# Issuing each 512-wide split product as two 256-wide matmuls per term

## The chip, the cores and the metric

The kernel runs on one core of a Trainium2 chip. The metric is the device time of one execution in microseconds (us), taken as the median of repeated runs. Of the engines, TensorE carries nearly all of this kernel's work: in the profile its matmuls stand as PE and its loads of the stationary operand as PEld. VectorE is DVE, ScalarE is ACT, GpSimd is POOL and SyncE is SP.

## The reference, cut to what matters

The reference is a two-layer encoder trunk on a sequence of 1024 tokens with 1024 features, all in float32:

```
h = h + mixer_ab(rmsnorm(h, g1), ...)      # layer 0: projections, chunked attention, output projection
h = h + dense_swiglu(rmsnorm(h, g2), ...)  # (silu(h @ w_gate) * (h @ w_up)) @ w_down, 2816 hidden
h = h + mixer_c(rmsnorm(h, g1), ...)       # layer 1: gated MLP with 128x128 position mixing
h = h + moe_swiglu(rmsnorm(h, g2), ...)    # top-2 of 8 experts, 3584 hidden each
return rmsnorm(h, final_norm)
```

Nearly all of the arithmetic is in products of an activation matrix with a weight matrix.

## The kernel before, in words

A float32 matrix product is computed from operands that are split in two. ScalarE copies a tile into a high part of type fp32r (`hi_part`, L271, tile `wh` of the raw weights `wraw`), and VectorE subtracts that from the original to give a low part (`lo_part`, L275, tile `wl`). Activations are split in the same manner, into `xh`/`xl` for the projections, `xdh`/`xdl` and `ah`/`al` for the dense layer, `exh`/`exl` and `mah`/`mal` for the experts. The helper `product` then issues three matmuls into one PSUM bank: high times high (L280), high times the low part of the moving operand (L281), and low stationary times high moving (L282). The first two have the same stationary tile of 128 by 128. The kernel issues no load of the stationary tile by itself; every matmul brings its own, which the profile shows as one PEld row for each PE row.

The stages follow one another on TensorE: value projection (`values_pe`, the moving operand is 512 columns of the weights), key and query projections (`half_pe`, 512 tokens), attention steps with further calls of `half_pe` between them (`attend_pe`), output projection (`out_proj_pe`), the dense layer in two halves of 512 tokens (`gate_up_pe` and `down_pe` with n = 512), the gated MLP (`mix_pe`), routing (`route_pe`), and then the experts one after another (`item_pe`, with the same `gate_up_pe` and `down_pe`). The number of tokens n that an expert's products move is one of `WIDTHS` = 240, 256, 272, 288, 304, 336, 384; `by_width` runs one loop over experts for each width. In this input the widths 240 (three experts), 256 (two), 288 (two) and 304 (one) occur. No expert's product is 512 columns wide, and the position mixing in `mix_pe` moves 128.

`gate_up_pe` is a hardware loop whose body holds four weight units of eight products each; `down_pe` has a loop of four units of eight products, with the first and the last units outside it. In `down_pe` the hidden tile is selected by a register, and the program computes the addresses on TensorE's sequencer. Weights come on SP's queue in units of 128 by 1024 into four slots; a slot is freed by `unit_used`, which the last matmul of a unit increments.

Of the kernel before, what the change touches and what calls it, by code (L numbers as in the profile page):

```python
# [58 lines left out]
def build(nc, io):  # L59
    ctx = ExitStack()  # L60
    with ctx:
# [211 lines left out]
        def lo_part(dve, q, j):  # L273
            dve.wait_ge(hi_done, 4 * q + j + 1)
            dve.tensor_tensor(wl[:, j], wraw[:, j], wh[:, j].bitcast(F32),  # L275
                              ALU.subtract).then_inc(lo_done, 1)

        def product(pe, out, a_hi, a_lo, b_hi, b_lo, first, last):

            pe.matmul(out, a_hi, b_hi, start=first, stop=False)  # L280
            pe.matmul(out, a_hi, b_lo, start=False, stop=False)  # L281
            return pe.matmul(out, a_lo, b_hi, start=False, stop=last)  # L282

        def wtile(w, j, k):
            return w[:, j, k * P:(k + 1) * P]
# [52 lines left out]
        def proj_qk_pe(pe, q, j, b, ready=None, order=tuple(range(KD))):  # L338
            pe.wait_ge(lo_done, 4 * q + j + 1)
            for half in range(2):  # L340
                c = slice(half * HALF, half * HALF + HALF)
                for i, k in enumerate(order):
                    if ready:
                        ready(half, i)
                    mm = product(pe, bank(b + half), wtile(wh, j, k), wtile(wl, j, k), xh[:, k, c], xl[:, k, c],
                                 i == 0, i == KD - 1)
                mm.then_inc((bank_full, unit_used)[half], 1)
# [31 lines left out]
        def values_pe(pe):  # L379
            for g in range(2):  # L380
                for j in range(4):
                    pe.wait_ge(lo_done, j + 1)
                    for kk in range(2):
                        k = 2 * j + kk
                        pe.wait_ge(n_lo, 8 * g + k + 1)
                        for t in range(4 * g, 4 * g + 4):
                            c = slice(t * P, t * P + P)
                            w = slice(512 * kk, 512 * kk + 512)
                            mm = product(pe, bank(t), xh[:, k, c], xl[:, k, c], wh[:, j, w], wl[:, j, w], k == 0, k == KD - 1)
                            if k == KD - 1 and t < 4 * g + 3:  # L390
                                mm.then_inc(v_mm, 1)
                    if g == 1 and j < 3:
                        mm.then_inc(unit_used, 1)
                    elif j == 3:
                        mm.then_inc((v_mm, unit_used)[g], 1)

        def half_pe(pe, u, half, b, ks, used=1):

            c = slice(half * HALF, half * HALF + HALF)
            for k in ks:  # L400
                mm = product(pe, bank(b), wtile(wh, u % 4, k), wtile(wl, u % 4, k), xh[:, k, c], xl[:, k, c], k == 0, k == KD - 1)
            if KD - 1 in ks:
                if half == 0:
                    mm.then_inc(first_half, 1)
                else:
                    mm.then_inc(unit_used, used)
# [1323 lines left out]
```

## Time and profile before

| quantity | before |
|---|---|
| median of 3 runs | 3862.95 us (3862.63 to 3863.59) |
| span of the profiled execution, first to last instruction | 3857.8 us |
| PE busy | 3631.9 us, 94% |
| PEld busy | 3247.7 us, 84% |
| DVE busy, ACT busy | 1724.7 us, 1645.1 us |
| PE matmuls, and weight loads | 24240, 24240 |

No separate time is recorded for the profiled execution: its span is 5.2 us less than the median, and that is what lies around it. Matmuls are pipelined, so the duration of one (its start to its modelled end) is longer than the distance from its start to the start of the next. A duration of 394 ns and a distance of 233 ns stand beside each other in one stage; how fast TensorE works is told by the distance alone. In a view by windows, the figure in brackets counts the instructions that touch the window.

### The profile page before, as it was taken

The numbers are of one execution on the slowest core, as the hardware profiler recorded it, in microseconds if no ns is written. First come the engines' busy times: TensorE is split into PE (matmuls) and PEld (weight loads), VectorE is DVE, ScalarE is ACT, GpSimd is POOL, SyncE is SP. The second block draws the span as 40 slices with busy tenths as digits, with TensorE's granted clock in tenths as the row PEclk, the third lists the DMA queues.
The fourth block names the chain that finished last, engine by engine and source line by source line (L and its number), as shares of the span: only waits on it lengthen the run. The fifth ranks groups of instructions, "written<-read, shape, count | busy, mean of one in ns | idle before, by whom it ended". The sixth has DMA issues, their size and how long they took to land.

```text
span 3857.8 us, 66155 instructions
## 1 busy us (share of the span) xinstructions
PE 3631.9 (94%) x24240; PEld 3247.7 (84%) x24240; DVE 1724.7 (45%) x2452; ACT 1645.1 (43%) x2290; POOL 100.0 (3%) x132
## 2 busy tenths in 40 slices
PE   8999899998999889977999999999999999999993
PEld 5777668886888677747999999999999999999993
DVE  4455433323332433344545555455554544544444
ACT  3455323323332322134546555564654544544542
POOL 1000000000000000010000000000000000000001
PEclk9999999999999999988999999999999999999997
DMA  5111312222222210146666666666565555555446
GB/s 173 34 52 42 115 55 92 92 93 71 93 96 94 104 55 33 55 81 201 193 205 191 206 193 198 201 191 206 191 195 175 164 166 177 164 167 171 158 155 235
DMA packets 150283, 533.85 MB, mean 138 GB/s; under 512 B 17976, under 2 KB 18016, under 8 KB 149936
## 3 DMA queue, kind: packets, MB, share of 16 engines
q1 hardware_dynamic: 126288, 459.86, 36.7%
q0 software_dynamic: 14624, 55.52, 4.0%
q10 hardware_dynamic: 9280, 17.24, 1.5%
q8 instruction: 60, 0.98, 0.1%
q14 instruction: 31, 0.25, 0.0%
HBM read 502.93 MB, written 33.28 MB: 139 GB/s over the span
## 4 chain that ended last, share of the span: by engine, by line
PE 91%; DVE 3%; ACT 2%; DMA 2%; issue 1%; POOL 0%; ACTq 0%; POOLq 0%; DVEq 0%
PE ps L280 29%; PE ps L282 28%; PE ps L281 28%; PE ps L329 1%; PE ps L521 1%; PE ps L506 1%; PE ps L1285 1%; PE ps L460 1%; DMA y<-yrow_d,slot 0%; PE ps L1314 0%; PE ps L541 0%; PE ps L529 0%; PE ps L1079 0%; DVE rstd L311 0%; DMA tok_d<-tokid,slot 0%
## 5 line engine op out<-in xcount | busy, mean ns | idle before, releaser
L275 DVE TENSOR_TENSOR wl<-wraw,wh 128x1024 fp32r<-128x1024 f32 x860 | 1052.1, 1224 | 1558.1 <-ACT wh L271 1558.1
L271 ACT ACTIVATE wh<-wraw 128x1024 fp32r<-128x1024 f32 x860 | 904.4, 1057 | 1197.5 <-PE ps L282 1189.1
L280 PE MATMUL ps<-exh,wh 128*128 128x240 f32 (+3 forms) x3584 | 1021.1, 285 | 11.9 <-issue 9.6
L282 PE MATMUL ps<-exh,wl 128*128 128x240 f32 (+3 forms) x3584 | 1022.2, 285 | 0.0
L281 PE MATMUL ps<-exl,wh 128*128 128x240 f32 (+3 forms) x3584 | 1018.6, 284 | 0.0
L280 PEld LDWEIGHTS ps<-exh,wh 128*128 128x128 f32 x3584 | 679.1, 189 | 12.8 <-issue 12.8
L281 PEld LDWEIGHTS ps<-exl,wh 128*128 128x128 f32 x3584 | 678.4, 189 | 0.0
L282 PEld LDWEIGHTS ps<-exh,wl 128*128 128x128 f32 x3584 | 677.5, 189 | 0.0
L282 PE MATMUL ps<-mah,wl 128*128 (+4 forms) x1792 | 510.5, 285 | 0.0
L280 PE MATMUL ps<-mah,wh 128*128 (+4 forms) x1792 | 509.8, 284 | 0.6
L281 PE MATMUL ps<-mal,wh 128*128 (+4 forms) x1792 | 509.2, 284 | 0.0
L280 PEld LDWEIGHTS ps<-mah,wh 128*128 128x128 f32 x1792 | 338.9, 189 | 2.5 <-issue 2.5
L282 PEld LDWEIGHTS ps<-mah,wl 128*128 128x128 f32 x1792 | 337.9, 189 | 0.0
L281 PEld LDWEIGHTS ps<-mal,wh 128*128 128x128 f32 x1792 | 337.8, 189 | 0.0
L843 ACT ACT_TABLE_LOAD x134 | 171.9, 1283 | 293.9 <-PE ps L282 270.1
L280 PE MATMUL ps<-xdh,wh 128*128 128x512 f32 x704 | 280.9, 399 | 14.9 <-DVE xdl L316 14.9
L281 PE MATMUL ps<-xdl,wh 128*128 128x512 f32 x704 | 279.1, 396 | 0.0
L282 PE MATMUL ps<-xdh,wl 128*128 128x512 f32 x704 | 279.1, 396 | 0.0
L280 PE MATMUL ps<-xh,wh 128*128 128x512 f32 x608 | 249.4, 410 | 19.5 <-DVE xl L773 5.6
L281 PE MATMUL ps<-xl,wh 128*128 128x512 f32 x608 | 243.5, 401 | 0.0
L282 PE MATMUL ps<-xh,wl 128*128 128x512 f32 x608 | 243.2, 400 | 0.0
L280 PEld LDWEIGHTS ps<-xdh,wh 128*128 128x128 f32 x704 | 132.5, 188 | 54.2 <-issue 14.7
(282 smaller groups left out, 3763.3 us busy)
## 6 DMA issues: line engine op xcount, KB each, us to landing
wraw<-in_w_expert SPq DMA_DIRECT2D x676, 512.0 KB, 3.9
wraw<-in_w_main SPq DMA_DIRECT2D x184, 512.0 KB, 3.2
yrow_d<-yst ACTq DMA_DIRECT2D x16, 512.0 KB
yT<-in_xT POOLq DMA_DIRECT2D x4, 1024.0 KB, 11.3
hT<-in_xT POOLq DMA_DIRECT2D x1, 4096.0 KB, 15.3
h_d<-hT POOLq DMA_DIRECT2D x1, 4096.0 KB, 13.2
hT<-h_d POOLq DMA_DIRECT2D x1, 4096.0 KB, 12.4
xrow_d<-rows ACTq DMA_DIRECT2D x16, 256.0 KB, 2.6
```

The source lines that it names most:

```text
L271: act.activation(wh[:, j], wraw[:, j], ACT.Copy).then_inc(hi_done, 1)
L275: dve.tensor_tensor(wl[:, j], wraw[:, j], wh[:, j].bitcast(F32), ALU.subtract).then_inc(lo_done, 1)
L280: pe.matmul(out, a_hi, b_hi, start=first, stop=False)
L281: pe.matmul(out, a_hi, b_lo, start=False, stop=False)
L282: return pe.matmul(out, a_lo, b_hi, start=False, stop=last)
L329: pe.matmul(sums(n), ones[:], sq[:, k % 2], start=k == 0, stop=k == KD - 1).then_inc(n_squ, 1)
L460: mm = pe.matmul(ps[:, starts[h] + a * P:starts[h] + b * P], (qAh, qAh, qAl)[part][hp, tc], key, start=part == 0, stop=part == 2)
L506: mm = pe.transpose(ps[:, o:o + P], eA[:, h, kk * P:kk * P + P], ident[:])
L521: mm = pe.matmul(Y_OUT[h * HD:h * HD + HD], v, ptA[:, kk, h], start=kk == 0, stop=kk == na - 1)
L843: act.activation(buf[:, par, 0:n], bank(par, n), ACT.Silu).then_inc(silu_done, 1)
L1285: mm = pe.transpose(bank(k % 4, P, P * s_), xg[:, s_, k * P:k * P + P], ident[:])
```

## The change

`product` still computes the same three terms in the same order into the same bank. When the moving operand has 512 columns, each term is issued as two matmuls of 256 columns, to the two halves of the bank, with the same stationary tile. Any other width is issued as before. Only the very first matmul of a sum carries `start`, and only the last `stop`.

```
+        COLS = 256
+
         def product(pe, out, a_hi, a_lo, b_hi, b_lo, first, last):
 
-            pe.matmul(out, a_hi, b_hi, start=first, stop=False)
-            pe.matmul(out, a_hi, b_lo, start=False, stop=False)
-            return pe.matmul(out, a_lo, b_hi, start=False, stop=last)
+            n = b_hi.shape[-1]
+            w = COLS if n == 2 * COLS else n
+            for part in range(3):
+                a, b = ((a_hi, b_hi), (a_hi, b_lo), (a_lo, b_hi))[part]
+                for c in range(0, n, w):
+                    s = slice(c, c + w)
+                    mm = pe.matmul(out[:, s], a, b[:, s], start=first and part == 0 and c == 0,
+                                   stop=last and part == 2 and c + w == n)
+            return mm
```

On TensorE, at the head of the dense layer's gate and up loop, two products of the kernel before stand as follows (`xdh` and `xdl` are the split activations, `wh` and `wl` the split weights):

```order
L280 MATMUL ps<-xdh,wh 128x512
L281 MATMUL ps<-xdl,wh 128x512
L282 MATMUL ps<-xdh,wl 128x512
L280 MATMUL ps<-xdh,wh 128x512
L281 MATMUL ps<-xdl,wh 128x512
L282 MATMUL ps<-xdh,wl 128x512
```

With the change the same two products, on the same engine at the same place, are these (x2 is two alike in a row):

```order
L288 MATMUL ps<-xdh,wh 128x256 x2
L288 MATMUL ps<-xdl,wh 128x256 x2
L288 MATMUL ps<-xdh,wl 128x256 x2
L288 MATMUL ps<-xdh,wh 128x256 x2
L288 MATMUL ps<-xdl,wh 128x256 x2
L288 MATMUL ps<-xdh,wl 128x256 x2
```

Six matmuls have become twelve, in the same order of terms, and nothing else was moved. In the dense layer's down loop the tiles `ah` and `al` are picked by a register. Before, the first product of a hidden tile on TensorE reads:

```order
L280 ISA
L280 MATMUL ps<-ah,wh 128x512
L281 REGISTER_ALU
L281 MATMUL ps<-al,wh 128x512
L282 MATMUL ps<-ah,wl 128x512
```

With the change it reads, at the same place of the down loop on TensorE:

```order
L288 ISA
L288 MATMUL ps<-ah,wh 128x256
L288 ISA
L288 MATMUL ps<-ah,wh 128x256
L288 REGISTER_ALU
L288 MATMUL ps<-al,wh 128x256
L288 REGISTER_ALU
L288 MATMUL ps<-al,wh 128x256
L288 MATMUL ps<-ah,wl 128x256 x2
```

The second half of each operand has an address of its own to compute, so the two sequencer instructions of a hidden tile have become four, beside twice as many matmuls.

## Rows read from the trace of the kernel before

**Rows 1.** The page: busy time, and the chain that ended last.

```profile
PE 3631.9 (94%) x24240; PEld 3247.7 (84%) x24240; DVE 1724.7 (45%) x2452; ACT 1645.1 (43%) x2290; POOL 100.0 (3%) x132
...
PE 91%; DVE 3%; ACT 2%; DMA 2%; issue 1%; POOL 0%; ACTq 0%; POOLq 0%; DVEq 0%
```

**Rows 2.** Groups by line and shape, PE: busy, mean ns of one | idle before.

```profile
L280 PE MATMUL ps<-xdh,wh 128*128 128x512 f32 x704 | 280.9, 399 | 14.9 <-DVE xdl L316 14.9
...
L281 PE MATMUL ps<-xl,wh 128*128 128x512 f32 x608 | 243.5, 401 | 0.0
...
L280 PE MATMUL ps<-exh,wh 128*128 128x256 f32 x896 | 247.6, 276 | 1.1 <-DVE wl L275 1.1
...
L281 PE MATMUL ps<-al,wh 128*128 x256 | 100.9, 394 | 0.0
...
L281 PE MATMUL ps<-wl,xh 128*128 128x512 f32 x192 | 77.3, 403 | 0.0
...
L281 PE MATMUL ps<-al,wh 128*128 128x512 f32 x96 | 37.8, 394 | 0.0
```

**Rows 3.** The timeline of PE in the dense layer, 512 columns.

```profile
1000.01 0.39 PE L280 MATMUL ps<-xdh,wh 128*128 128x512 f32 x1
1000.24 0.39 PE L281 MATMUL ps<-xdl,wh 128*128 128x512 f32 x1
1000.48 0.39 PE L282 MATMUL ps<-xdh,wl 128*128 128x512 f32 x1
```

**Rows 4.** The timeline of PE in an expert, 256 columns.

```profile
2600.02 0.28 PE L280 MATMUL ps<-exh,wh 128*128 128x256 f32 x1
2600.13 0.28 PE L281 MATMUL ps<-exl,wh 128*128 128x256 f32 x1
2600.24 0.28 PE L282 MATMUL ps<-exh,wl 128*128 128x256 f32 x1
```

**Rows 5.** Windows in which PE never stops: busy (x count) of each engine.

```profile
core 0: us, PE busy (x) PEld busy (x) DVE busy (x) ACT busy (x) POOL busy (x), PEclk, DMA share, GB/s
446.00:470.00 24.00, 24.00 (x105) 19.34 (x104) 8.01 (x10) 2.13 (x2) 0.00 (x0) 1.00 0.21 66
560.00:780.00 220.00, 220.00 (x944) 176.38 (x943) 73.60 (x79) 73.87 (x88) 0.00 (x0) 1.00 0.29 95
790.00:860.00 70.00, 70.00 (x302) 56.12 (x301) 17.09 (x17) 13.76 (x13) 0.00 (x0) 1.00 0.29 97
45.00:65.00 20.00, 20.00 (x90) 16.39 (x89) 16.26 (x21) 6.88 (x12) 4.31 (x7) 1.00 0.25 58
1346.00:1372.00 26.00, 26.00 (x115) 21.36 (x114) 11.20 (x16) 7.40 (x9) 1.05 (x2) 1.00 0.24 81
1800.00:1900.00 100.00, 100.00 (x885) 100.00 (x884) 56.91 (x74) 61.14 (x83) 0.00 (x0) 1.00 0.62 195
2490.00:2620.00 130.00, 130.00 (x1150) 130.00 (x1149) 74.73 (x96) 80.30 (x109) 0.00 (x0) 1.00 0.61 193
2628.00:2660.00 32.00, 32.00 (x285) 32.00 (x284) 14.59 (x13) 12.59 (x12) 0.00 (x0) 1.00 0.63 196
3240.00:3390.00 150.00, 150.00 (x1128) 150.00 (x1127) 76.13 (x96) 80.86 (x106) 0.00 (x0) 1.00 0.50 163
```

**Rows 6.** Who PE waited for: us in total, times, longest.

```profile
PE ps L280 <- DVE xdl L316: 14.9, 7, 6.5
...
PE ps L280 <- issue: 9.6, 2, 6.2
...
PE ps L521 <- ACT ptA L657: 9.4, 7, 2.8
```

**Rows 7.** Groups by line, PEld: the loads of the dense layer's gate and up.

```profile
L280 PEld LDWEIGHTS ps<-xdh,wh 128*128 128x128 f32 x704 | 132.5, 188 | 54.2 <-issue 14.7 <-DVE xdl L316 7.7
```

**Rows 8.** DMA queues from 1985 to 2470 us, and in the whole span.

```profile
q1 hardware_dynamic: 25029, 91.14, 58.8%
q0 software_dynamic: 928, 3.15, 2.0%
q10 hardware_dynamic: 1088, 2.10, 1.3%
...
q8 instruction: 60, 0.98, 0.1%
```

## The prediction

> **What bounds the kernel now.** I read the page first. PE is busy for 3631.9 of 3857.8 us, DVE and ACT for less than half, and 91% of the chain that ended last is PE [rows 1]. So the time is the time in which TensorE gets through its matmuls, and the change has to be costed in matmuls of two widths.
>
> The groups by shape give the count. Each of the three lines of `product` has 704 matmuls of 512 columns on `xdh` or `xdl`, 608 on `xh` or `xl`, 256 + 96 on `ah` or `al`, and 192 with the weights moving [rows 2]. That is 1856 products, three times 1856 = 5568 matmuls of 512 columns, out of 24240. The rest are the experts' and the small ones, which the change leaves alone.
>
> The same groups tempt to a wrong price. One matmul of 512 columns lasts 394 to 403 ns and one of 256 lasts 276 [rows 2], and by these two for one would cost about 150 ns more, or some 840 us in all. But these are durations from start to modelled end and they overlap. The timeline shows a start every 0.23 us in the dense layer [rows 3] and every 0.11 us in an expert of 256 columns [rows 4]. The distance between starts is what counts.
>
> To get it finer than the timeline I take windows in which PE never stops [rows 5]. An instruction is counted in a window if it touches it, so the distance is (length of the window + duration of one) / count:
>
> - Dense gate and up, 512 columns: 220.394 / 944 = 233.5 ns. Dense down: 70.394 / 302 = 233.1 ns. I take 233.4.
> - Output projection, 512 columns of `xh`: 24.4 / 105 = 232.4 ns.
> - Weights moving, 512 columns: 20.4 / 90 = 226.7 ns in layer 0, 26.4 / 115 = 229.6 in layer 1. I take 228.2.
> - Expert of 256 columns: gate and up 130.276 / 1150 = 113.3 ns, down 32.276 / 285 = 113.2.
> - Expert of 240 columns: 100.277 / 885 = 113.3 ns. Expert of 288: 150.297 / 1128 = 133.2 ns.
>
> Two things are to be seen in them. The 256-wide matmul comes every 113.3 ns, and twice that is 226.6, less than the 233.4 of one 512-wide. And at 240 columns the distance is no smaller than at 256, while PEld is busy for the whole window there, against 176.38 of 220 us at 512. Something that comes once for each matmul, most likely the load of the stationary tile, sets a floor of 113.3 ns.
>
> **The change part by part.** It removes 5568 matmuls of 512 columns and adds 11136 of 256, each with its load. No row shows a 256-wide pair on one stationary tile in a split product, but its parts are shown. L280 and L281 already follow each other on the same stationary tile `wh`, and the 256-wide windows hold these steps with the others: the mean over all three is 113.3 ns, and in the timeline the step from L280 to L281 is the same 0.11 us as the one from L281 to L282 [rows 4]. So I price the pair at 2 x 113.3 = 226.6 ns.
>
> - Dense layer: 3 x (704 + 352) = 3168 matmuls, each 233.4 - 226.6 = 6.8 ns less: 21.5 us.
> - `xh` moving: 3 x 608 = 1824, each 232.4 - 226.6 = 5.8 ns less: 10.6 us. Some 500 of these stand in the attention steps (`half_pe` is called there for 21 half units of 8 products, 504 matmuls), where a gain may turn into waiting for `ptA`; that wait is 9.4 us in total now, in 7 places [rows 6], and 500 x 5.8 ns = 2.9 us is all that could be lost so. I take off 1.
> - Weights moving: 3 x 192 = 576, each 1.6 ns less: 0.9 us.
>
> The sum is 32 us less. Against the profiled execution that gives 3857.8 - 32 = 3826 us of span, and with the 5.2 us around it 3831 for the median.
>
> The bounds of the pair: below, the nearest row is the floor that 240 columns share with 256, and the pair has two loads, so 226 is the least that a row supports; if the gain also reaches the weight-moving products and 233.5 holds for `xh`, it is some 8 ns each, 45 us. Above, the 288-wide row: a line through 288 (133.2 ns) and 512 (233.4) rises by 100.2 / 224 = 0.447 ns for a column and gives 118.9 at 256, so a pair of 237.8. I take the measured 256 since it is the width itself, with the same operand types, helper and loop, in gate and up as well as in down.
>
> The page "TensorE: Matmul & The Clock Gate" of the Trainium skill, section "The mechanism" (of packing small matmuls), says that a load of weights overlaps with running matmuls only when it goes to another group of rows. By that each added load would stand in the open, as in the last rival below. The trace disagrees: in the 256-wide window PE and PEld are both busy for all 130 us [rows 5], and 113.3 ns between starts is less than the 188 ns that one load lasts [rows 7].
>
> Costed at nothing: the sequencer instructions of the down loop double together with its matmuls, and the experts' down loop has the same ratio at 113.2 ns between starts [rows 5]. The waits stay where they are, since every increment sits on the last matmul of the same unit. The end of a sum, which DVE and ACT wait for, comes at 113 + 276 = 389 ns after the start of the last pair, against 394. The clock is granted in full (1.00) at 256 columns as at 512 [rows 5]. Weights are asked for at 95 GB/s in the dense layer and 193 in the experts, so the queue has room for a TensorE that goes 3% faster. The norms that PE waits for (14.9 us, [rows 6]) are DVE's and stay.
>
> **The rivals.**
>
> *The cost goes by columns.* The 512-wide matmul takes 0.456 ns for a column where the experts' 256 takes 0.443. If that 3% belongs to how the tiles lie in memory and not to the width, the 256-wide halves take 116.7 ns each and nothing changes: 3863. For it speaks that at one width the distance differs between stages (226.7, 229.6, 232.4, 233.4), so that placement has a say. Against it, that gate and up and down of the 256-wide expert, on different tiles, agree to 0.1 ns.
>
> *A fixed cost for each matmul.* This is the line above: 118.9 ns at 256 columns. The 3168 then cost 4.4 ns more each, 13.9 us; the 1824 cost 5.4, 9.8 us; the 576 cost 9.6, 5.5 us. Together 29 us slower: 3892. It decides as soon as a half comes at more than 116.7 ns. For it: both 288 and 512 lie on such a line, and so does common sense about issuing twice as often. Against it: the 256-wide row is 5.6 ns under the line. The same page of the Trainium skill, section "Back-to-back issue gap", gives a warm distance of N / 2.4 + 2.5 ns; as an estimate from it a pair of 256 costs 2.5 ns more than one of 512, 14 us over all 5568, which is this rival in a smaller size. Its 215.8 ns for 512 columns is not what the window shows.
>
> *The loop bodies become too long.* The gate and up loop turns 11 times for each half, 20 turns back in all, and its body doubles in matmuls. If each turn back had to fetch code anew, the nearest price is the 6.2 us of the longest "issue" wait [rows 6], which stands where TensorE goes over to the loop of the next width: 20 x 6.2 = 124 us, 3987. Against it: from 1985 to 2470 us TensorE runs two more whole experts of 240 columns, a loop body much longer than that one, and no packet of the instruction queue q8 stands among the queues of that stretch, with 60 in the whole span [rows 8]. The Trainium skill's page "Runtime: NRT & Kernel Launch", section "Instruction fetch mechanics", speaks of a window of two pages and of a stall at a branch out of it; these rows show no such refetch.
>
> *The added load is exposed after all*, because both halves use the tile that is in the array. 5568 x 188 ns [rows 7] = 1047 us, 4910. L280 and L281 share a tile and show nothing of it [rows 4].
>
> **How the numbers follow.** Forecast 0.60, by columns 0.15, fixed cost 0.17, loop bodies 0.06, exposed load 0.02. The likeliest case by itself lies between 3816 (45 us and a little) and 3844 (placement takes away half). The range has to take in no change and, to hold 8 in 10, the nearer half of the fixed cost: 3815 to 3886. A difference of 0.2%, 7.7 us, is about what the measurement can tell from no change. Faster by more: nearly all of the forecast and a little of the column case, 0.61. Same: 0.15. Slower: 0.24.
>
> **What the changed profile would show.** PE x29808 and PEld x29808. In the dense layer's windows one 256-wide matmul every 113.3 ns, PEld busy for the whole window as in the experts, and the two halves of the dense layer about 11 us shorter each. If the distance there is 116 to 117, the column case holds; at 119 the fixed cost. Gaps at the turn of the gate and up loop with q8 packets between them would show the third rival. The experts' stretch should keep its length. Wrong would be the forecast if the 256-wide expert tiles owe their 113.3 ns to their place in memory.

## The result and the profile after

| | before | changed |
|---|---|---|
| median | 3862.95 us (3856.97 to 3870.69, 7 runs) | 3833.62 us (3827.89 to 3866.08, 7 runs) |
| ratio, 95% interval | | 0.9945 (0.9926 to 0.9964) |
| span of the profiled execution | 3857.8 us | 3826.1 us |

The changed kernel is faster by 0.55%. The predicted 3831 us is 2.6 us from the median, and the profiled span is the 3826 us that the sum gave. Both are met in part by luck, as the stages and the runs below show. But the runs of the changed kernel spread over 38 us, and the ratio speaks of 21 us where the medians differ by 29 and the spans by 32. (The kernel before spread over 14 us in these runs, over 26 in twenty-three later ones and over 23 in thirty more.) Where the changed kernel's spread comes from is what the experiments had to tell.

The page of the changed kernel, its busy times, the chain that ended last and the queue that fetches instructions:

```profile
PE 3599.4 (94%) x29808; PEld 3484.0 (91%) x29808; DVE 1724.0 (45%) x2452; ACT 1644.5 (43%) x2290; POOL 99.8 (3%) x132
...
q8 instruction: 80, 1.31, 0.1%
...
PE 91%; DVE 4%; ACT 2%; issue 2%; DMA 1%; POOL 1%; ACTq 0%; POOLq 0%; DVEq 0%
```

Against [rows 1], 5568 matmuls and as many loads have been added, PE is busy for 32.5 us less, and the chain is PE's as before. The windows of the changed kernel answer to [rows 5] (busy and count of PE, PEld, DVE, ACT, POOL, then granted clock, DMA share and GB/s):

```profile
560.00:780.00 220.00, 220.00 (x1944) 220.00 (x1943) 76.39 (x82) 75.74 (x91) 0.00 (x0) 1.00 0.31 96
450.00:470.00 20.00, 20.00 (x179) 20.00 (x178) 4.80 (x6) 1.79 (x2) 0.00 (x0) 1.00 0.20 60
45.00:65.00 20.00, 20.00 (x172) 20.00 (x171) 15.71 (x20) 6.23 (x11) 3.72 (x6) 1.00 0.26 66
1320.00:1346.00 26.00, 26.00 (x223) 26.00 (x222) 12.11 (x16) 6.89 (x9) 1.05 (x2) 1.00 0.22 72
```

By the same formula as ahead, (length + duration) / count with a duration of 276 ns, the distance is 113.3 ns in the dense layer, 113.3 in the output projection, and 117.9 and 117.8 where the weights move. PEld is busy for the whole window, as in the experts. The last two rows are the first deviation: a pair there costs 235.7 ns where one whole matmul cost 228.2.

What the dense layer gave is read from its first and last matmul. Before (PE, minimum, median and maximum duration, first and last start):

```profile
L280 PE MATMUL ps<-xdh,wh x704: 393/394/767, 535.3 to 1179.2; 128*128 128x512 f32 x176
L282 PE MATMUL ps<-ah,wl x352: 393/394/397, 786.4 to 1302.9; 128*128 x128, 128*128 128x512 f32 x48
```

The same two rows of the changed kernel:

```profile
L288 PE MATMUL ps<-xdh,wh x1408: 276/276/553, 532.3 to 1158.0; 128*128 128x256 f32 x176
L288 PE MATMUL ps<-ah,wl x704: 276/276/276, 776.5 to 1278.1; 128*128 x128, 128*128 128x256 f32 x48
```

From 535.3 to 1302.9 it took 767.6 us, from 532.3 to 1278.1 it takes 745.8: 21.8 us less, where 21.5 were forecast. All that stands ahead of the dense layer gave 3.0 us (535.3 - 532.3). From the dense layer's last matmul to the experts' first it is 2.2 us less (1302.9 to 1765.1, and 1278.1 to 1738.1). The last 4.7 us lie from there to the end, in code that the change does not touch. Of the dense layer's 21.8 us, 20.6 lie in its two halves, 10.3 each, and 1.2 in the norm between them.

The 4.7 us can be read from the trace too. A 240-wide stretch of an expert's gate and up products of the kernel before, and the first such stretch of the changed kernel (PE alone):

```profile
1800.00:1900.00 100.00, 100.00 (x885) 1.00 0.62 195
1773.00:1873.00 100.00, 100.00 (x895) 1.00 0.61 197
```

That is 113.3 ns before and 100.275 / 895 = 112.0 ns now, for the same instructions. Before, two of the three 240-wide gate and up stretches stood at 113.3 ns, which costs 1344 x 1.3 ns = 1.7 us each, and one 256-wide down stretch at 117.8 ns instead of 113.3, which costs 336 x 4.5 ns = 1.5 us. In the profile of the changed kernel none of them did. So 31.7 us less in the span is 27.0 us in the stages that the change touches and 4.7 us in the experts, which no term of the sum has.

One pair of traces doesn't fix the small terms. Two more profiles of the changed kernel and one of the kernel before are among the runs below. The dense layer began at 535.3 and 540.9 us in the two profiles of the kernel before, and at 532.3, 534.5 and 533.3 in the three of the changed kernel. From its first to its last matmul it took 767.6 and 764.9 us before, and 745.8, 745.7 and 745.8 with the change. The dense gain is well clear of that spread; the 3.0 and the 2.2 us are not.

### The profile page after: what moved, and what is told of

Its sections match the earlier page's. It is cut to its first block, busy times and chain, and to the rows that moved or that the text cites. A ratio compares the mean times of both kernels' runs of the same rounds, so it can differ in the third digit from the quotient of the medians.

```text
span 3826.1 us, 77419 instructions
## 1 busy us (share of the span) xinstructions
PE 3599.4 (94%) x29808; PEld 3484.0 (91%) x29808; DVE 1724.0 (45%) x2452; ACT 1644.5 (43%) x2290; POOL 99.8 (3%) x132
## 4 chain that ended last, share of the span: by engine, by line
PE 91%; DVE 4%; ACT 2%; issue 2%; DMA 1%; POOL 1%; ACTq 0%; POOLq 0%; DVEq 0%
PE ps L288 85%; PE ps L337 1%; PE ps L529 1%; PE ps L514 1%; PE ps L468 1%; PE ps L1293 0%; PE ps L1322 0%; DMA y<-yrow_d,slot 0%; PE ps L549 0%; PE ps L537 0%; PE ps L1087 0%; DVE rstd L319 0%; POOL tok_d L1269 0%; DMA tok_d<-tokid,slot 0%; PE ps L492 0%
## 5 line engine op out<-in xcount | busy, mean ns | idle before, releaser
L288 PE MATMUL ps<-xdh,wh 128*128 128x256 f32 x1408 | 277.9, 279 | 14.3 <-DVE xdl L324 14.1
L288 PE MATMUL ps<-xdl,wh 128*128 128x256 f32 x1408 | 276.2, 278 | 0.0
L288 PE MATMUL ps<-xdh,wl 128*128 128x256 f32 x1408 | 276.1, 278 | 0.0
L288 PE MATMUL ps<-xh,wh 128*128 128x256 f32 x1216 | 247.1, 285 | 20.0 <-DVE xl L781 5.9
L288 PE MATMUL ps<-xl,wh 128*128 128x256 f32 x1216 | 241.0, 280 | 0.0
L288 PE MATMUL ps<-xh,wl 128*128 128x256 f32 x1216 | 240.1, 279 | 0.0
L288 PEld LDWEIGHTS ps<-xdh,wh 128*128 128x128 f32 x1408 | 213.8, 189 | 16.9 <-issue 14.7
```

What stands on the lines that cost most here:

```text
L288: mm = pe.matmul(out[:, s], a, b[:, s], start=first and part == 0 and c == 0, stop=last and part == 2 and c + w == n)
```

## The experiments

**Terms by half.** Is it the twice repeated stationary tile that makes the pair cheap or dear? The loops are turned, so that all three terms are issued for one half of the columns and then for the other.

```
-            for part in range(3):
-                a, b = ((a_hi, b_hi), (a_hi, b_lo), (a_lo, b_hi))[part]
-                for c in range(0, n, w):
+            for c in range(0, n, w):
+                for part in range(3):
+                    a, b = ((a_hi, b_hi), (a_hi, b_lo), (a_lo, b_hi))[part]
```

> All three terms for columns 0 to 255, then all three for 256 to 511, so that the same number of 256-wide matmuls is issued but only the first two of three share a stationary tile. If the distance between starts is set by the width and the load alone (my theory): dense layer 113.3 ns as in the changed kernel, value products 117.8 ns as there, span within 3 us of the changed kernel's. If a tile that is loaded twice in a row costs or saves something: the dense distance moves by over 1 ns, some 11 us of span for each ns, or the value products come down to 113.3 ns.

Median 3854.32 us over 12 runs (3832.06 to 3860.96), 0.997 of before (0.9952 to 0.9987). The windows of its profile, one in each half of the dense layer:

```profile
560.00:780.00 220.00, 220.00 (x1944) 220.00 (x1943) 76.04 (x81) 75.50 (x91) 0.00 (x0) 1.00 0.31 95
960.00:1180.00 220.00, 220.00 (x1870) 220.00 (x1869) 72.30 (x77) 71.96 (x86) 0.00 (x0) 1.00 0.31 93
```

The first half stands at 113.3 ns, as in the changed kernel. The second, with the same instructions in the same loops, stands at 220.276 / 1870 = 117.8 ns. So the order of the terms is not what makes the cheap distance; it exists in both. And there are two distances for one and the same stream of 256-wide matmuls. Neither theory had that. The span came out at 3853.5 us, 27 over that of the changed kernel where 3 was the bound. The dense layer accounts for 12.3 of the 27; its output projection stood at 117.8 ns too, and 5.1 us lie in the experts, which the edit leaves alone.

**The moving weights whole.** The value products of layer 0 and the v part of layer 1 are issued in 512 columns again.

```
-            w = COLS if n == 2 * COLS else n
+            w = COLS if n == 2 * COLS and not whole else n
```

> The change without the products whose moving operand is the weights (values in layer 0 and the v part in layer 1, 576 matmuls of 512 columns whole again). My theory: these go back from a pair at 2 x 117.8 = 235.6 ns to 228.2, the others keep 113.3, so the span is 576 x 7.4 ns = 4.3 us shorter than the changed kernel's, about 3822. Rival: the value stretches wait for something else (norm, loads), and the span does not move.

Median 3850.51 us over 12 runs (3828.12 to 3862.83), 0.9967 (0.9946 to 0.9987). Its profile, in the value products and in both halves of the dense layer:

```profile
560.00:780.00 220.00, 220.00 (x1870) 220.00 (x1870) 72.30 (x77) 73.57 (x88) 0.00 (x0) 1.00 0.29 91
960.00:1180.00 220.00, 220.00 (x1944) 220.00 (x1943) 75.81 (x82) 76.81 (x92) 0.00 (x0) 1.00 0.31 98
50.00:70.00 20.00, 20.00 (x89) 16.43 (x88) 12.33 (x18) 6.88 (x11) 2.73 (x4) 1.00 0.25 79
```

The value products went back to 20.4 / 89 = 229.2 ns, as expected. But this time the first half of the dense layer is the one at 117.8, and that outweighs the 4 us. The span of 3847.8 us is 22 over the changed kernel's where 4.3 under it was expected; 13.9 of the 22 lie in the dense layer. The changed kernel was not timed beside these two, so whether their code meets 117.8 ns more often than its code does is not shown.

**128 columns.** `COLS` is 128, so each 512 is issued as four.

> Four matmuls of 128 columns for each 512. Floor for each matmul and its load (my theory): 113.3 ns each or a little less (109), a 512 in 436 to 453 ns, 5568 x (436 to 453 - 233.4) = 1128 to 1223 us over the kernel before, 4990 to 5086 us. Cost by columns: 58 ns each, 3863 us. Fixed cost of 4.4 ns and 0.447 ns for a column: 61.6 ns each, 5568 x 13 = 73 us more, 3936 us.

It took 7134 us, far outside all three. A window in the dense layer, PE alone (busy, count, granted clock, DMA share, GB/s):

```profile
1200.00:1400.00 200.00, 200.00 (x939) 0.50 0.07 24
```

Here the granted clock is 0.50, the lower of the two levels (1.2 GHz), and the distance (200 + 0.415) / 939 = 213 ns. The number at full clock, which was the purpose, isn't given by this stage. The same trace has it elsewhere. From 407 to 748 us, in the attention steps, the granted clock was 1.00, and the projections there ran in groups of 48 matmuls between shorter ones. A window in one of them, and its timeline (rows of four matmuls each):

```profile
437.50:442.00 4.50, 4.50 (x43) 1.00 0.01 2
437.61 0.61 PE L288 MATMUL ps<-xl,wh 128*128 128x128 f32 x4
438.06 0.61 PE L288 MATMUL ps<-xh,wl 128*128 128x128 f32 x4
```

Four matmuls take 0.45 us, and from start to start within the groups of this stretch the mean is 112 ns at 128 columns. That is inside the 109 to 113.3 of the floor, where cost by columns would give 58 and the small fixed cost 61.6: both fall at full clock. The 3270 us over the kernel before are this floor, paid for the greater part at the lower clock.

**288 and 224 columns.** The same count of matmuls as in the change, cut unevenly.

```
-                for c in range(0, n, w):
-                    s = slice(c, c + w)
+            cuts = (0, 288, n) if n == 512 else (0, n)
+                for c, e in zip(cuts[:-1], cuts[1:]):
+                    s = slice(c, e)
```

> Each 512 as 288 and 224 columns. Floor (my theory): 133.2 + 113.3 = 246.5 ns for the pair, 5568 x (246.5 - 233.4) = 73 us over the kernel before, about 3936 us. Cost by columns: no change, 3863. Fixed cost: 237.8 ns, 3887 us. With the floor the PEld row is busy all the time only in the 224 part.

3943 us, against 3936 forecast. Both windows of its dense layer count the same, at full clock:

```profile
600.00:900.00 300.00, 300.00 (x2434) 300.00 (x2434) 89.40 (x93) 84.71 (x98) 0.00 (x0) 1.00 0.29 88
```

That is 300.3 / 2434 = 123.4 ns on average, 246.8 for the two, against 246.5 from adding the experts' 133.2 and the floor of 113.3. It is the measurement that parts the theories: cost by columns would have given 233.4, the fixed cost 237.8. A 224-wide matmul doesn't get the time back that it saves in columns. One part of the expectation was wrong: PEld was busy for the whole window, in the 288-wide part as well.

**The changed kernel and the one before, once more.** Is each half's distance fixed by the code?

> The changed kernel once more, for its profile. In the profiles so far a 256-wide stretch of the dense layer runs through at one of two distances, 113.3 ns or 117.8. If the distance is fixed by the code and the placement of the tiles, this profile has 113.3 in both halves of the dense layer and a span of 3826 us. If it is settled anew each time that a stretch begins, each half has either, and the span is 3826 us plus some 14 us for each half at 117.8.

> The kernel before once more, for its profile. Its 512-wide stretches stood at 233.3 ns in both halves of the dense layer. If 512-wide matmuls have two distances as well, one half or both are at another value here; if not, 233.3 again, the halves 377 and 394 us from norm to norm as before, and the span differs only by the experts.

The changed kernel again had 113.3 ns in both halves (x1943 in each of the two windows) and took 3832.54 us with a span of 3830.7. Either reading allows that, so this run didn't decide between them. The kernel before took 3866.71 us, and its windows in the two halves were

```profile
560.00:780.00 220.00, 220.00 (x945) 177.25 (x944) 72.27 (x77) 73.85 (x88) 0.00 (x0) 1.00 0.27 93
960.00:1180.00 220.00, 220.00 (x944) 176.31 (x943) 73.85 (x79) 74.42 (x90) 0.00 (x0) 1.00 0.27 93
```

that is 233.2 and 233.5 ns. In four profiled halves the 512-wide matmul has shown one distance, and PEld is idle for a fifth of the time there. Two distances have been seen in streams in which PEld never rests: 113.3 and 117.8 ns at 256 columns, and 112.0 and 113.3 at 240. The span of the kernel before was 7.2 us longer than in its first profile, and not by the experts alone as expected: 5.6 us of it lie ahead of the dense layer.

**Half the load in the experts' down products.** Is the load of the stationary tile the floor? The run is made on the kernel before.

```
-                        mm = product(pe, bank(b + d, n), wh[:, j, c], wl[:, j, c], rh, rl,
+                        m = P if n == HALF else P // 2
+                        mm = product(pe, bank(b + d, n)[0:m], wh[:, j, c][:, 0:m], wl[:, j, c][:, 0:m], rh, rl,
```

> The kernel before, with only the first 64 of 128 stationary columns in the experts' down products, so half of each expert's output rows is left out; widths and counts of matmuls stay. If the load of the stationary tile makes the floor at 240 and 256 columns (my theory), the distance there falls from 112 to 113.3 ns to somewhere between the streaming time of the columns, 240 or 256 at 0.417 ns, and that: 101 to 109; at 288 and 304 columns it stays at 133.3 and 138.7. If each matmul has a fixed cost whatever it loads, nothing moves.

Windows in the down products of its experts: two of 240 columns, two of 256, one of 288.

```profile
1925.00:1955.00 30.00, 30.00 (x274) 30.00 (x272) 14.21 (x12) 11.66 (x11) 0.00 (x0) 1.00 0.61 203
1965.00:1995.00 30.00, 30.00 (x284) 30.00 (x283) 13.49 (x11) 12.65 (x12) 2.91 (x3) 1.00 0.81 263
2625.00:2655.00 30.00, 30.00 (x267) 30.00 (x265) 13.51 (x12) 11.68 (x11) 0.00 (x0) 1.00 0.60 196
2670.00:2700.00 30.00, 30.00 (x254) 30.00 (x253) 12.71 (x11) 11.62 (x11) 0.37 (x1) 1.00 0.70 240
3140.00:3170.00 30.00, 30.00 (x230) 30.00 (x229) 12.26 (x10) 9.80 (x10) 0.00 (x0) 1.00 0.50 170
```

At 240 columns the distance is 110.5 and 106.6 ns, less than the 112.0 and 113.3 that this width shows with the whole load, and inside the expected 101 to 109 in one of the two. At 256 columns it is 113.4 and 119.2, so half the load bought nothing. At 288 it is 131.7, where 133.2 was to stay. The load has a part in the floor at 240 columns: five of the six 240-wide down stretches stood at 110.6 to 110.8 ns, one at 106.8. At 256 my reading that the load sets the 113.3 ns is refuted. What sets it there, the stream of the columns or a cost that each matmul has, is not shown. A second distance exists with half the load too, at 119.2 ns.

**A stop at each unit.** Where is the distance settled? In the dense gate and up loop, TensorE waits before each unit for its own last one.

```
+                if n == HALF:
+                    pe.wait_ge(unit_used, 4 * q + j)
```

> The changed kernel, where TensorE waits in the dense gate and up loop before each unit until its own unit before has ended, so the stream stops 87 times. If the distance is settled where a stream starts and kept until it stops, single units stand at 113.3 and others at 117.8 ns within one half. If it depends on something that lasts longer (the half's data or placement), all units of a half have the same. The stops themselves cost some 0.3 us each, about 26 us.

3897.0 us. The dense layer took 802.3 us, 56.6 more than in the profile of the changed kernel taken beside it, where 26 were expected. By the starts in the trace the 86 stops within the loop took some 30 us, the slower first step behind each some 7, and stretches at 117.8 ns some 19. The timeline of PE over one of the stops (start, duration, rows of two matmuls each):

```profile
602.43 0.39 PE L288 MATMUL ps<-xdh,wh 128*128 128x256 f32 x2
602.66 0.39 PE L288 MATMUL ps<-xdl,wh 128*128 128x256 f32 x2
602.89 0.39 PE L288 MATMUL ps<-xdh,wl 128*128 128x256 f32 x2
603.38 0.47 PE L288 MATMUL ps<-xdh,wh 128*128 128x256 f32 x2
603.69 0.40 PE L288 MATMUL ps<-xdl,wh 128*128 128x256 f32 x2
603.92 0.40 PE L288 MATMUL ps<-xdh,wl 128*128 128x256 f32 x2
604.16 0.40 PE L288 MATMUL ps<-xdh,wh 128*128 128x256 f32 x2
604.40 0.40 PE L288 MATMUL ps<-xdl,wh 128*128 128x256 f32 x2
```

Ahead of the stop pairs start 0.23 us apart, behind it 0.24 (and between the first two rows 0.31). The counts are sharper. The windows 604 to 609 and 598 to 603 of this run:

```profile
604.00:609.00 5.00, 5.00 (x45) 1.00 0.28 85
598.00:603.00 5.00, 5.00 (x47) 1.00 0.42 130
```

5.276 / 45 = 117 and 5.276 / 47 = 112 ns, as near as five microseconds can tell. Over the 86 starts behind such stops, the mean distance within a unit is either 113.3 (41 units) or 117.8 (45), and nothing between, in one execution of one program. So the distance is settled where a stream starts, and the data and tile placement of a half are not what chooses. Chance alone doesn't choose either. Of the 44 starts behind the shortest stops (0.38 us from the start of the last matmul to that of the next) 33 ran on at 117.8; of the 42 behind stops of 0.5 to 0.7 us 30 ran on at 113.3. To the nanosecond, as the trace stores the starts, the split is complete:

| last start before the stop to first start behind it | starts | ran on at |
|---|---|---|
| 380 and 384 ns | 33 | 117.8 |
| 385 ns | 11 | 113.3 |
| 515 to 520 ns | 22 | 113.3 |
| 529 and 530 ns | 10 | 117.8 |
| 630 and 631 ns | 8 | 113.3 |
| 636 and 677 ns | 2 | 117.8 |

No length is seen with both distances, and a few nanoseconds part them. The unit ahead of the stop goes with it too: behind one at 113.3 ns all 30 of the short stops led to 117.8, behind one at 117.8 ns 11 of 14 led to 113.3. Whether the length chooses the distance, or shows a choice that something else has made, is not shown.

**One stop in each half.** If the start sets the distance for all that follows, a single short stop can decide half of the dense layer. The first turn of the loop gets a loop of its own, and one unit in it has the wait.

```
+            for lo, hi in ((0, 1), (1, nf // 2)):
+                with pe.Fori(lo, hi) as i:
+                    for r in range(4):
+                        body(i + (q0 + (phi + r) // 4), (phi + r) % 4, 2 * i + r // 2, lo == 0 and r == 2)
```

> The changed kernel with one stop for each half of the dense layer: TensorE waits before the third unit of the first turn of the gate and up loop until its own second unit has ended. In the run with a stop at every unit, all starts after such a stop at that place of the turn ran on at 113.3 ns. If the start of a stretch sets its distance, both halves of the dense layer stand at 113.3 ns from there to their end in this profile, the stops cost about 0.4 us each, the span is near 3827 us and the slow runs of the changed kernel (3843 to 3866 us) become rarer. If it is chance at every start, the two halves are mixed as before.

The second kernel has `r == 1` in this line.

> The same with the one stop before the second unit of the first turn instead, where the starts ran on at 117.8 ns in nearly every case. If the start sets the distance, both halves stand at 117.8 ns from there on: some 14 us more for each half, a median near 3855 to 3860 us, 25 us or so over the kernel with the stop before the third unit, though both stop once. By chance at every start: the same time as the other kernel.

The third has the stop of the first, and the moving weights whole.

> The stop before the third unit, and the products with moving weights issued whole: the version that both findings point to. Value products at 227 to 231 ns again for 512 columns instead of 2 x 117.8, 3 to 4 us less than with the stop alone, a median near 3825 us.

The changed kernel was timed beside them.

> The changed kernel once more, on the same chip as the three others, to compare them with. If each half's distance is settled by chance at its start, the runs spread from 3828 to 3860 us in steps of some 14 us, with a median near 3835.

| kernel | median (lowest to highest) | ratio to before | distances, halves 1 and 2 |
|---|---|---|---|
| changed | 3834.56 (3830.96 to 3859.47) | 0.9935 (0.9910 to 0.9959) | 113.3, 113.3 |
| stop before the third unit | 3869.62 (3861.67 to 3876.51) | 1.0014 (1.0002 to 1.0027) | 117.8, 117.8 |
| stop before the second unit | 3872.47 (3858.35 to 3878.20) | 1.0012 (0.9997 to 1.0027) | 117.8, 117.8 |
| stop before the third, weights whole | 3863.73 (3857.35 to 3872.34) | 0.9997 (0.9985 to 1.0010) | 117.8, 117.8 |

The timeline of the kernel with the stop before the third unit shows the place:

```profile
546.39 0.39 PE L288 MATMUL ps<-xdl,wh 128*128 128x256 f32 x2
546.62 0.39 PE L288 MATMUL ps<-xdh,wl 128*128 128x256 f32 x2
547.11 0.47 PE L288 MATMUL ps<-xdh,wh 128*128 128x256 f32 x2
547.42 0.40 PE L288 MATMUL ps<-xdl,wh 128*128 128x256 f32 x2
547.66 0.40 PE L288 MATMUL ps<-xdh,wl 128*128 128x256 f32 x2
```

and its windows what became of it, more than 200 us later and in the other half:

```profile
560.00:780.00 220.00, 220.00 (x1870) 220.00 (x1869) 72.72 (x78) 73.40 (x89) 0.00 (x0) 1.00 0.31 93
960.00:1180.00 220.00, 220.00 (x1870) 220.00 (x1869) 72.27 (x77) 73.78 (x88) 0.00 (x0) 1.00 0.30 92
```

My expectation of the first kernel was wrong and its mechanism right. I had taken the place of the unit in the turn for the cause. In the run with a stop at every unit the third unit's stops had lasted 0.52 us. Here, with no stop ahead of it, the stop before the third unit came out short (380 ns, 0.27 us more than no stop), like those that all gave 117.8, and so it did, in both halves, and stayed for more than two thousand matmuls. The second kernel's stops were 384 and 380 ns and gave 117.8 as well. Its expectation had a row read wrongly: of the 22 starts at the second unit 11 had run on at 117.8 ns, ten in the first half and one in the second; it was the fourth unit that had it in all 22. With both kernels at 117.8, the comparison of the two that the expectation was after fell away.

The stops themselves cost under 1 us, and the median of the first kernel is 35 us over that of the changed one on the same chip. Between the two profiled runs the spans differ by 31.2 us: 28.0 of them lie in the dense layer, as 3168 pairs at 9.0 ns more would have it, and 6.5 in the experts, where the first 256-wide one stood at 117.8 ns throughout; the stages between gave a little back. The third kernel has a median 5.9 us under the first, near the 3 to 4 expected of the whole weights; their intervals overlap a little. It beats neither the changed kernel nor, clearly, the one before, and 3825 us was expected of it.

## Why the prediction was right, by its own steps

*PE bounds the kernel, 5568 matmuls become 11136.* Right, to the count.

*The distance between starts is the price, not the duration.* Right, and it decided the sign: durations of 394 and 276 ns would have told of 840 us more.

*The pair costs 2 x 113.3 = 226.6 ns, by the row of the same width.* Right for the dense layer in all three profiles of the changed kernel: 21.8 us against 21.5, of which 20.6 lie in the two halves. It was incomplete in one point. The 256-wide stream has a second distance of 117.8 ns, so a pair can also cost 235.6, 2.2 more than one of 512. My rows had the second distance in reach, in one of the experts' down stretches that I had not windowed. With it, 226.6 is the lower of two prices and not their mean: a half of the dense layer at 117.8 costs 1584 x 9.0 ns = 14 us more. The run of terms by half with one such half took 3855.3 us, that of the whole weights with one 3849.4, and the three profiled runs of the changed kernel with none 3827.9, 3832.5 and 3832.9. The dense layer gives 12 to 14 us of these differences, and the rest lies in other stages. That the changed kernel's other runs between 3843 and 3866 us had such halves is likely by this; they have no trace. Nor is the spread all the change's: the kernel before has 256-wide and 240-wide experts with two distances and spreads over 14 to 26 us.

*Weights moving, 0.9 us less.* Mis-sized and of the wrong sign: 576 x (235.7 - 228.2) = 4.3 us more, since both value stretches stood at 117.8 and 117.9. (The 226.7 ns of layer 0 was also a reading error: in a window of 20 us one count more or less is 2.5 ns, and the second profile of the kernel before counts 89 there, 229.2 ns.) It is the second distance again, not a property of those products: in the kernel with the stop before the third unit the same window counts 179 matmuls, 113.3 ns.

*`xh` moving, 9.6 us less.* The distance of the output projection was right (113.3). Together with the value products' part, the sum gave 5.4 us for the stretch up to the dense layer: 672 + 384 matmuls at 5.8 ns, 192 at 1.6 ns, and 1 us taken off. The stretch gave 3.0 in the first profile. The value products account for 192 x 9.1 ns = 1.7 us of the 2.4 that lack, and the rest is less than this stretch varies from one profile to the next. In the attention steps the changed kernel has both distances side by side.

*The sum, 3826 us of span and 3831 of median.* The terms came out at 27.0 us in place of 32 in the stages that they are about; 4.7 us from the experts, at nothing in the sum, made up for it. That is luck. So is part of the 3831: the 5.2 us laid around the span were 1.7 to 1.8 us in every run that lists both. With them the sum gives 3828, which the profiled run met (3827.9), and the median of 3833.6 is 6 us above.

*A floor that comes with each matmul, most likely the load.* A floor: shown by the uneven cut, 246.8 ns against 246.5, and by 112 ns at 128 columns. Its size of 113.3 ns at 240 columns was the upper of that width's two distances; the other is 112.0. The load: refuted at 256 columns, partly right at 240.

*The rivals.* Cost by columns fell with the uneven cut. The fixed cost of 118.9 ns fell with it and with the dense rows, though the second distance comes within 1.1 ns of it, so that a price close to it was real and its mechanism not. As for the Trainium skill's rule (page "TensorE: Matmul & The Clock Gate", section "The mechanism") that a load overlaps with a running matmul only in another group of rows, no window of the changed kernel shows an exposed load; PE and PEld are both busy for 220 of 220 us. Loop bodies: 80 packets on q8 against 60, no pause in the windows of the loop, where the page "Runtime: NRT & Kernel Launch" of the Trainium skill, section "Instruction fetch mechanics", would allow for stalls at the turns.

What stays open is what in a start selects one distance or the other. The length of the stop goes with it to the nanosecond in the 86 starts of one run, and no run set that length on purpose. Whether a start could be made that always gives 113.3 was tried once, at the wrong place, and not settled. The changed kernel is the fastest that I have found.

## What to carry to other kernels

Price a matmul by the distance between starts in a window where PE never stops, from a row of the same width, and look at every such stretch, since one width can have two distances. A long stream that is bound by matmuls and loads alike keeps the distance with which it started: a short wait in it can cost some fifty times its length (0.27 us of stop in a half, 14 us of half), and a single profile says which state it was in, not which one is usual. The price of a width is not to be had from a line through others: the one through 288 and 512 columns misses the 113.3 ns of 256 by 5.6. And compare the stages that a change leaves alone as well: here they gave 4.7 of 31.7 us.

## What the hardware showed that I had not expected

- 256-wide fp32r matmuls with a load each start every 113.3 or every 117.8 ns, for hundreds of microseconds without change, in the same code and the same run. At 240 columns the two are 112.0 and 113.3. 512-wide ones stood at 233 to 234 ns in the dense layer in each profile.
- With 128 columns for each load the granted clock stood at 0.50 in the dense layer, though PE and PEld were busy without a pause, and a matmul came every 213 ns; in the attention steps of the same run it stood at 1.00 for 341 us, and one came every 112. With 256, 288 and 224, and 512 columns it was 1.00 in the windows shown here. The cut into 128 cost 3270 us.
- Halving the stationary tile made a 256-wide matmul no cheaper where it came every 113.4 ns, and did not lower the second distance either (119.2).
